# Dividing the input chunks between the score levels of an HGRN stage by token blocks

## The reference, cut to what matters

```python
h = x @ w_in[l]                                  # 1024 -> 2560
u = h[..., :D_POOL]
q, f_raw, v, g = jnp.split(h[..., D_POOL:], 4, axis=-1)
y_pool = multiscale_pool(u, pool_w[l], pool_scale[l])
o = hgrn2_recurrence(q, f_raw, v, lb_all[l])     # o_t = S_t^T q_t, S_t = diag(f_t) S_{t-1} + (1-f_t) outer v_t
y_hgrn = head_rms_norm(o, hgrn_norm_g[l]) * jax.nn.silu(g)
mix = jnp.concatenate([y_pool, y_hgrn], axis=-1) @ w_out[l]
x = layer_norm(ALPHA_2 * x + mix, ln_g[l, 1], ln_b[l, 1])
```

## Time and profile before

| | us |
|---|---|
| median of 3 runs | 2418.55 |
| lowest, highest | 2409.77, 2421.46 |
| profiled execution, device time | 2419.57 |
| its span | 2417.6 |
| TensorE busy | 2214.3 (92%) |
| VectorE busy | 1076.5 (45%) |
| ScalarE busy | 734.3 (30%) |

### The profile page before, as it was taken

The page is one execution under the profiler, slowest core; times in us unless marked ns, Lnnn a source line. Parts: engine busy times, 40 slices in busy tenths (PEclk is TensorE's granted clock), DMA queues, the critical chain, the costliest instruction groups (busy, mean ns, idle before and its releaser), DMA issues.

```text
span 2417.6 us, 32311 instructions
## 1 busy us (share of the span) xinstructions
PE 2214.3 (92%) x13534; PEld 1641.1 (68%) x13534; DVE 1076.5 (45%) x1606; ACT 734.3 (30%) x1123; POOL 60.4 (2%) x62
## 2 busy tenths in 40 slices
PE   7978998799898889978988999988999999888998
PEld 7874443343377845424433899888998999788997
DVE  4663221121167722211212655666556555666555
ACT  3432110011134321101111444443444444543443
POOL 0010000000010100000000000001000000001000
PEclk9989999899997799999999999989999999979999
DMA  9437999999962389999999746523554565423551
GB/s 295 132 141 313 420 421 421 417 420 420 400 205 69 133 328 420 421 420 416 420 421 401 242 165 209 161 84 114 183 192 163 186 209 192 140 70 116 181 192 52
DMA packets 231548, 622.79 MB, mean 258 GB/s; under 512 B 15456, under 2 KB 166944, under 8 KB 182112
## 3 DMA queue, kind: packets, MB, share of 16 engines
q1 hardware_dynamic: 225952, 604.99, 66.1%
q0 software_dynamic: 3040, 10.78, 1.3%
q10 hardware_dynamic: 2400, 4.83, 0.6%
HBM read 619.51 MB, written 1.05 MB: 257 GB/s over the span
## 4 chain that ended last, share of the span: by engine, by line
PE 42%; DMA 6%; DVE 4%; ACT 1%; issue 1%; SPq 0%; POOL 0%; DVEq 0%; ACTq 0%
PE bank L228 28%; PE bank L1486 9%; PE bank L1326 3%; DMA wide_tables<-in_moe_w_up 1%; DMA x_tok<-in_moe_w_up 1%; DMA ring<-in_moe_w_up 1%; DMA w_parts<-in_moe_w_up 1%; DMA ring<-in_ffn_gate 1%; PE bank L1647 1%; DVE w_low L429 1%; DVE x_tok L674 0%; DVE x_tok L663 0%; DVE bn L652 0%; PE bank L469 0%; ACT w_high L422 0%
## 5 line engine op out<-in xcount | busy, mean ns | idle before, releaser
L429 DVE TENSOR_TENSOR w_low<-ring,w_high 128x1024 fp32r<-128x1024 f32 x364 | 440.6, 1225 | 374.2 <-ACT w_high L422 374.1
L228 PE MATMUL bank<-xT_high,w_high 128*128 128x256 f32 x1712 | 488.3, 285 | 20.4 <-DVE xT_low L491 12.0
L228 PE MATMUL bank<-xT_low,w_high 128*128 128x256 f32 x1712 | 486.5, 284 | 0.0
L228 PE MATMUL bank<-xT_high,w_low 128*128 128x256 f32 x1712 | 486.2, 284 | 0.0
L422 ACT ACTIVATE w_high<-ring 128x1024 fp32r<-128x1024 f32 x364 | 376.6, 1052 | 296.2 <-PE bank L228 274.6
L1326 PE MATMUL bank<-ring,arena 128*64 128x512 f32 x1344 | 339.4, 594 | 18.2 <-DMA ring<-in_moe_w_up 6.0
L228 PEld LDWEIGHTS bank<-xT_high,w_high 128*128 128x128 f32 x1712 | 330.2, 193 | 26.1 <-DVE xT_low L491 12.0
L228 PEld LDWEIGHTS bank<-xT_low,w_high 128*128 128x128 f32 x1712 | 330.4, 193 | 2.8
L228 PEld LDWEIGHTS bank<-xT_high,w_low 128*128 128x128 f32 x1712 | 330.3, 193 | 0.0
L1326 PE MATMUL bank<-w_parts,arena 128*64 128x512 f32 x768 | 259.1, 596 | 14.4 <-DMA w_parts<-in_moe_w_up 6.6
L1326 PEld LDWEIGHTS bank<-ring,arena 128*64 128x64 f32 x1344 | 111.2, 137 | 230.5 <-issue 221.6
(11 more groups left out here) (285 smaller groups left out, 2860.4 us busy)
## 6 DMA issues: line engine op xcount, KB each, us to landing
ring<-in_moe_w_gate SPq DMA_DIRECT2D x56, 1024.0 KB, 23.6
ring<-in_moe_w_up SPq DMA_DIRECT2D x56, 1024.0 KB, 22.7
ring<-in_moe_w_down SPq DMA_DIRECT2D x56, 1024.0 KB, 26.1
ring<-in_ffn_gate SPq DMA_DIRECT2D x44, 1024.0 KB, 5.7
ring<-in_ffn_up SPq DMA_DIRECT2D x44, 1024.0 KB, 5.4
ring<-in_ffn_down SPq DMA_DIRECT2D x44, 1024.0 KB, 5.3
w_parts<-in_moe_w_down SPq DMA_DIRECT2D x32, 1024.0 KB, 26.6
w_parts<-in_moe_w_gate SPq DMA_DIRECT2D x32, 1024.0 KB, 22.1
```

Of the source, the lines that this page charges most:

```text
L228: ins = e.matmul(out, lhs, rhs, start=first and i == 0, stop=last and i == len(parts) - 1)
L429: e.tensor_tensor(lo, src, hi.bitcast(F32), ALU.subtract).then_inc(*S.low.tell(key))
```

## The change

TensorE makes the products of chunks 6 to 9 block by block: block 0 of chunk 6 ahead of the levels as before, then one block behind each of the levels 8 to 2. The body of the loop over blocks in `project_pe` becomes a function of its own, and the bank is opened at a chunk's first block. ScalarE evacuates chunk 6 at step 2, 7 at step 4, 8 at step 6 and 9 at step 8, and it does so ahead of the split at the same step, where it split first before. VectorE's program is as it was.

```diff
@@ project_pe @@
     for tb in range(NB):
-        parts = []
-        for c in range(2):
-            _, hi, lo = split_views(k, key + (c,))
-            parts += block_products(k, tb, hi, lo, c * (KT // 2))
-        e.wait_ge(*S.low[key + (1,)])
-        if fresh is not None:
-            x_ready(e, k, fresh, tb)
-        ins = mm(e, bank[:, tb * 256:(tb + 1) * 256], parts)
-    ins.then_inc(*S.used.tell(key + (1,)))
+        project_block_pe(e, k, key, bank, tb, fresh)
+
+
+def project_block_pe(e, k, key, bank, tb, fresh=None):
+
+    S, parts = k.S, []
+    for c in range(2):
+        _, hi, lo = split_views(k, key + (c,))
+        parts += block_products(k, tb, hi, lo, c * (KT // 2))
+    e.wait_ge(*S.low[key + (1,)])
+    if fresh is not None:
+        x_ready(e, k, fresh, tb)
+    ins = mm(e, bank[:, tb * 256:(tb + 1) * 256], parts)
+    if tb == NB - 1:
+        ins.then_inc(*S.used.tell(key + (1,)))
@@ hgrn_pe @@
     def values(step):
-        if step in (0, 2, 4, 6):
-            project_pe(e, k, inp(6 + step // 2))
+        if step > 8:
+            return
+        n = max(step - 1, 0)
+        key = inp(6 + n // 2)
+        bank = k.banks.open(e, A_BANKS, key) if n % 2 == 0 else k.banks[key]
+        project_block_pe(e, k, key, bank, n % 2)
@@ hgrn_act @@
     def values(step):
+        if step in (2, 4, 6, 8):
+            c = 5 + step // 2
+            into(c, (b.v if c < 8 else b.gate)[:, :, 256 * (c % 2):256 * (c % 2) + 256])
         if step in (0, 2, 4, 6):
-            c = 6 + step // 2
-            split_after(c)
-            into(c, (b.v if c < 8 else b.gate)[:, :, 256 * (c % 2):256 * (c % 2) + 256])
+            split_after(6 + step // 2)
```

## The result

The changed kernel takes 2447.81 us (median of 4 runs, 2445.70 to 2450.63), the kernel before in the same comparison 2420.01 (4 runs). The ratio is 1.0124, with a 95% interval of 1.0091 to 1.0156. That is 27.8 us more; 29.7 were forecast, and 2448.2 us. The median nearly met the forecast one partly because the kernel before came out 1.5 us higher here than the 2418.55 that the forecast added to.

A forecast was written before the change was run, and what follows sets the result against it. TensorE, busy 92% of the span, was taken to bound the kernel; half-chunk work, standstills and start gains gave 4.05 us, low clock 25.6, together +29.7 on 2418.55: 2448.2 us, range 2430 to 2470.

The forecast's parts named there:

- The wait that appears: Before levels 7, 5 and 3, TensorE stands 4.8 us each, because ScalarE's split waits for the half chunk's end.
- Rival C: Faster: the next split is under way when the half ends, so VectorE doesn't stand; -12.8 us, 2406; chance 0.07.
- The levels 6, 4, 2 and 1: Half chunks ahead of these levels, 2.88 us of work, cover waits of at most 0.7, taken as gone.
- The clock: Low clock behind level 8 and three standstills costs 2.6 + 3 x 3.4 = 12.8 us a layer.
- L: One layer's low-clock loss from chunk 6's second half to the value products: 12.8 us, bounds 0 and 32.4.
- Rival B: Half chunks too short to bring the clock back before the next sparse place; 2459 to 2487 us; chance 0.15.
- The start: Level 8's exponentials no longer stand behind chunk 6's evacuation: gain 0.35 us in layer 0, 2.0 in layer 1.
- the upper bound of 3.1: Largest gain at layer 1's start, if the table load runs ahead and only VectorE's own work is left.
- the sum: Work, standstills, end wait and low clock, less the old stretches and start gains: 4.05 + 2L = +29.7 us.
- the middle stretches: From chunk 6's second half, behind level 8, to the value products: about 60.7 us long in each layer.
- The stretches behind: Feed-forward behind the stage keeps its length, later loads priced at nothing; a changed length would show the forecast wrong.

The follow-up runs named there:

- Experiments 1 and 3: 1: changed kernel with VectorE's low parts one level later, 2400.26 us; 3: changed kernel with ScalarE's split ahead of the evacuation again, 2446.89 us.
- Experiment 4: Changed kernel with busy matmuls on constants in the six standstills: 2437.35 us with 8 calls each, 2428.99 us with 5.
- experiment 2: Changed kernel with ScalarE's splits one level later and VectorE's low parts two levels later: 2397.32 us, run again 2397.13 us.

## Why the prediction was right

*The wait that appears.* Forecast 4.8 us before levels 7, 5 and 3, measured 4.63, six times (I had counted to the next possible start, the trace counts from the last matmul's end). Experiments 1 and 3 show both halves of the reason: VectorE's place makes the standstill, and the part buffers tie it to the half's end even without the evacuation. Rival C, which needed a split under way when the half ends, is out.

*The levels 6, 4, 2 and 1.* No waits before them, as forecast.

*The clock.* L forecast at 12.8 a layer, measured 13.9 and 13.0, or 13.4 and 12.5 if the standstills are counted as in the forecast, to the next possible start (4.79), at the forecast places: behind level 8 and the standstills. Experiment 4 shows that it was their consequence. The size rests on an analogy that might have failed: a low stretch of 3.4 us of loss, read behind waits under 0.5, was put behind waits of 4.8, and a standstill did cost 3.2 to 4.0 (level 7 with half 7a took 8.69 us, for 4.66 at the full clock; level 3 with 9a 7.87). Rival B, a clock that stays low because the halves are short, didn't come: the halves behind levels 6, 4 and 2 are at 2.4 GHz throughout. (The argument for it was weaker than written: of the 26 matmuls that the prediction read in the first low stretch 2 are level 8's, so 24 of chunk 7 ran low, no more than a half has.) The Trainium skill's account of bursts between waits ("TensorE: Matmul & The Clock Gate", "HAM oscillation — how this bites in real kernels") agrees with the trace in that each burst behind a standstill began low (level 7's products took 3.7 us for 1.9); but here the clock was back in every burst by the end of its first half, after 16 to 24 of its matmuls.

*The start.* Forecast -0.35 and -2.0, measured -0.33 and -2.87. The second was under-sized: the load of ScalarE's exponential table did not wait for the distances, but ran directly behind the split, well ahead of the first exponential, so the upper bound of 3.1 was nearer:

```profile
2136.63 1.28 ACT L1711 ACT_TABLE_LOAD   x1
2141.34 0.63 ACT L1711 ACTIVATE arena<-arena 128x512 f32<-128x512 f32 x1 [3.43 <-DVE arena L1695]
```

*Not in the sum.* The value products, which the sum left as they were, came behind a busy level 1 and ran at 2.4 GHz: in layer 0 the next product followed 2.7 us after their start (1649.61 to 1652.28). In the kernel before it was 5.1 (from 1634.34):

```profile
1639.45 0.54 PE L228 MATMUL bank<-w_high,xT_high 128*128 128x256 f32 x1
```

With what follows, the last stretch is 3.3 us shorter over both layers. This and the start's 0.9, against the middle stretches' +0.3 (121.7 for the forecast 121.4), make the difference between the forecast 29.7 and the 25.8 counted in the stage.

*The stretches behind.* The forecast priced later loads at nothing and named a changed length there as a sign of being wrong. Between the stages it is 1.9 us longer, and experiment 2's kernel shows either length in its two executions (474.8 and 477.2), so no cost of later loads is shown.

So the sum was right in its large terms and a little high by two small ones that leaned the same way. That the measured 27.8 lies nearer to it than the stage's 25.8 is due to what varied outside the stage, and is luck.

## What to carry to other kernels

Work that is cut into smaller pieces finishes later, and everything tied to its end moves with it: buffers come free later, and an engine that prepares the next piece then stands at a place in its program where something urgent is queued behind it. Before interleaving finer on one engine, list for every other engine what its next instruction waits for and what stands behind that; here taking the low parts one level later turned a loss of 28 us into a gain of 17. And a wait on TensorE is to be priced with the slower products behind it: here 4.6 us of standstill cost 3.2 to 4.0 more at the low clock.

## What the runs showed of the hardware that I had not expected

- An activation table load ran as soon as ScalarE's earlier instruction was done, and ended 3.4 us ahead of the exponential that needed it, while that still waited for VectorE (2136.63 and 2141.34 above).
- Small shifts of the levels change the clock by more than the waits they remove: moving only the evacuations took 0.5 us from the waits before levels in layer 0 but 3.7 from the stretch, and the granted clock rose from 0.77 to 0.84.
- A fill of 4.45 us in a standstill of 4.6 to 4.8 did not always hold the clock (16 low matmuls in half 9a of either layer), one of 7.03, which left no wait behind it, did in all six places.
